# The first block's seven products in another order

## The chip, the cores and the metric

One core of one Trainium2 chip. The metric is the device time of one execution in microseconds (us), from a launch to its end; the median of the runs shown is compared.

## The reference, cut to what matters

The kernel computes one trunk layer for 1024 frames of width 2048: an RMSNorm of x, one input projection, attention over windows of 128 frames, a short gated convolution, one output projection added to x, and a final RMSNorm.

```python
hn = rmsnorm(x, norm_w[l])
proj = einsum('bsd,de->bse', hn, w_in[l])          # 2048 -> 5376 columns
q, k, v, g_attn, h, c_gate, b_gate, g_conv = split(proj, SPLIT_POINTS)
attn = swa_sink_attention(q, k, v, sinks[l], rel_bias)
conv = short_gated_conv(h, c_gate, b_gate, conv_w[l], conv_b[l])
mixed = concatenate([attn * silu(g_attn), conv * silu(g_conv)])
x = x + einsum('bse,ed->bsd', mixed, w_out[l])
return rmsnorm(x, final_norm_w)
```

Everything is float32. What the change touches is the first of eight blocks, which makes `g_attn` (1024 columns) from `hn`.

## The kernel before

**Blocks and products.** All projections are done in eight blocks of 1024 output columns (the second one, QKV, has 1280). A block is a 2 x 2 times 2 x 2 product of halves, done by seven products in place of eight (a Strassen-like scheme in Winograd's form): products 1 and 2 take halves of the weights and of x as they are; 3, 5, 6, 7 and 4 take sums and differences of halves. For the weights these are `s1`, `s2`, `s4`, `s3`, for x `t1`, `t2`, `t3`, `t4`, each in four parts (argument q, 0 to 3). All are made by VectorE in place in the buffers `raw` (weights) and `z` (x). `s2(q)` needs `s1(q)`, `s4(q)` needs `s2(q)`, `s3(q)` needs `s4(q)`; likewise `t2` needs `t1`, `t3` needs `t2`, `t4` needs `t3`. Product 5 takes `s1` and `t1`; product 3 `s4` and the x half that `t2` later overwrites; 6 takes `s2` and `t2`; 7 `s3` and `t3`; 4 the weights as they are and `t4`.

**Steps.** A product is four steps, so a block has 28 and the run 224; step n of this text is the n of the code, and S(n) the time at which TensorE begins it. In the first block product 2 is steps 0 to 3, product 1 steps 4 to 7, and (before) 3 is 8 to 11, 6 is 12 to 15, 7 is 16 to 19, 5 is 20 to 23, 4 is 24 to 27. A step takes two slices of 128 rows, over four output tiles of 128 x 512 (five in QKV), with three matmuls each, since every operand is split into a high and a low float32r part: 24 matmuls (30 in QKV). The three matmuls are high by high, high by low, low by high.

**The splitting.** For each step ScalarE copies the two x slices (`x_hi`, indices 2n and 2n+1, L1007) and the weights (`w_hi`, L976), and VectorE subtracts to get the low parts (`x_lo`, L1349, and `w_lo`, L1336). These go into rings: three steps of weights (`w_ring`), five slices of x (`x_main`). In step n the two engines make `x(2n+3)`, `w(n+2)` and `x(2n+4)`; the ring lets `x(2n+3)` begin only when step n-1 is done, and TensorE needs `x_lo(2n+1)` and `w_lo(n)` to begin step n.

**Order by hand.** Each engine runs one list of instructions in program order; a loop over the steps and four quarters of each says what goes where. Tables at the top place the first block's other work: `S1_AT`, `S24_AT` (`s2` and `s4` together), `B21_AT`, `PARK_AT`, `PLACE1_AT`, `TURN1_AT`, `T1_AT`; `late` shifts `t2`, `t3`, `t4`; `s3` runs from step 12. An engine that waits in this list holds up everything behind it.

**x in the first block.** The first block also makes x itself: TensorE transposes raw x into banks (`turn_x0`, `turn_x1`), and VectorE (`place_0`, `t1_from_turn`) and ScalarE (`place_1`, L1046) move it to `z`. The first step after product 1 waits in `wait_bank` for all eight `place_1` and all eight `t1`. Every x slice of the first block from step 4 on is stored to `x_park` in DRAM by GpSimd's queue (L499), the first steps' slices by `park_hi`, `park_lo`, `store_park` (eight jobs, `PARK_AT`), and the following five blocks load x from there, one DMA of 1024 KB a step (`load_x`, L557). `load_x` of steps 28 and 29 goes to `x_far`.

**Banks.** Products 6 and 7 go on in the banks of product 1, so tile t of product 7 waits until VectorE has read product 6's tile t. Product 3 has banks of its own in the first block. After 2, 3 and 7 ScalarE copies the banks to `e` (`copy_out`, L1100); after 1, 6, 5, 4 VectorE adds or subtracts them (`sums`); product 5's tiles take two instructions each (L1500, L1502).

**The SP queue.** SyncE issues all loads in one list: the next block's weights into `raw` (16 DMAs of 512 KB a block, each when its part of `raw` is free, that is after a `w_lo`), `load_more` (four DMAs of 512 KB, `x_raw`: the extra 256 columns of QKV, needed at step 26 by `more_hi` and then `more_lo`, L1529), `store_gate` (1024 KB each), `load_x`. `load_more` goes into the space of x's low half, so it waits for the last `x_lo` of product 7. `tanh_gate` and `silu_gate` finish the gates, four pairs.

Of the kernel before, what the change touches and what calls it, by code (L numbers as in the profile page):

```python
# [9 lines left out]
ALU = mybir.AluOpType  # L10
# [44 lines left out]
BLOCKS = 8  # L55
ORDER = [(2, 1, 3, 6, 7, 5, 4)] + [(2, 1, 6, 7, 5, 3, 4)] * 5 + [(1, 2, 3, 6, 7, 5, 4), (2, 1, 6, 7, 5, 3, 4)]
AT = [{p: i for i, p in enumerate(o)} for o in ORDER]
# [13 lines left out]

COPIED = [(o[0], 3, 7) if b in ON_CHIP else (o[0], 6, 7) for b, o in enumerate(ORDER)]
ADDED = [(o[1], 6, 5, 4) if b in ON_CHIP else (o[1], 5, 3, 4) for b, o in enumerate(ORDER)]

# [18 lines left out]
def copy_count(b, p, t):  # L93
    return sum(3 * w for w in WIDE[:b]) + COPIED[b].index(p) * WIDE[b] + t + 1

# [13 lines left out]
def _banks():  # L109
    held, free, loose = {}, [0, 1, 2, 3, 4, 5], []  # L110
    for b in range(BLOCKS):
        if b == CONV0:
            free = [k for k in free + loose if k != 5]
            loose = []
        elif b == OUT0:
            free = free + loose + [5, 6, 7]
            loose = []
        for p in ORDER[b]:
            if (b, p) == (GATES, 3):
                free = free + [6, 7]  # L120
            if (b, p) == (QKV, 2):
                free = [k for k in free + loose if k < 6]
                loose = []
            goes_on = {6: 1, 7: 6}.get(p)
            if p == 3 and b not in ON_CHIP:
                goes_on = 5
            mine = []
            for t in range(WIDE[b]):
                if goes_on:
                    k = BANK[b, goes_on, t]  # L130
                else:
                    if t > 0 and loose:
                        free.append(loose.pop(0))
                    if not free:
                        free.append(loose.pop(0))
                    k = free.pop(0)
                BANK[b, p, t] = k
                BANK_BEFORE[b, p, t] = held.get(k)
                held[k] = (b, p, t)
                mine.append(k)  # L140
            free += loose
            loose = []
            if not (p in (1, 6) or (p == 5 and b not in ON_CHIP)):
                loose = mine
# [72 lines left out]
W_TABLED = 10  # L217
S1_AT = {(5, 0): 0, (7, 0): 1, (7, 2): 2, (8, 0): 3}
S24_AT = {(6, 1): 0, (7, 1): 1, (7, 3): 2, (8, 2): 3}
X_HI_AT = {(1, 0): (4, 5), (2, 0): (6, 7), (3, 2): (8, 9), (4, 0): (10,),  # L220
# [28 lines left out]
def build(nc, x, x_t, col_params, w_in, sinks, w_out, rel_bias, final_norm_w, one_hot, out):  # L249
    ctx = ExitStack()  # L250
    with ctx:
# [39 lines left out]
        squares = [z[:, 1, 2:4, :], raw[:, 1, 12:14, :], e[:, 0, 0:2, :], e[:, 0, 2:4, :]]  # L291
        park_stage = [e[:, i, 2 * j:2 * j + 2, :] for i in (1, 3) for j in range(2)]
        taps = cols[:, 0:(TAPS + 1) * GROUPS].rearrange("p (t g) -> p t g", t=TAPS + 1)
# [212 lines left out]
        def _(sp):  # L506
            def load_raw(b, c, j):

                k = slice(2 * j, 2 * j + 2)
                if b > 0:  # L510
                    p = {(0, 0): 7, (0, 1): 3, (1, 0): 5, (1, 1): 4}[c, j // QP]
                    sp.wait_ge(w_lo_ready, at(b - 1, p, j % QP) + 1)
                if b == GATES:
                    src = w_in_v[:, k, GATE_COL + c * N:GATE_COL + (c + 1) * N]
                elif b == QKV:
                    src = w_in_v[:, k, c * N:(c + 1) * N]
                elif b < OUT0:
                    m = b - CONV0
                    for r in range(2):
                        op = sp.dma_start(raw[:, c, k, r * 2 * P:(r + 1) * 2 * P],  # L520
                                          w_conv_v[:, k, 2 * c + r, m * 2 * P:(m + 1) * 2 * P])
                        if r == 0:
                            op.then_inc(raw_loaded[8 * c + j], 16)
                    op.then_inc(raw_loaded[8 * c + j], 16)
                    return
                else:
                    src = w_out_v[:, k, ((b - OUT0) * 2 + c) * N:((b - OUT0) * 2 + c + 1) * N]
                sp.dma_start(raw[:, c, k, :], src).then_inc(raw_loaded[8 * c + j], 16)
# [201 lines left out]
            for n in range(-3, STEPS):  # L730
# [6 lines left out]
                for quarter in range(4):  # L737
# [11 lines left out]
                    if b == GATES:  # L749
                        if (i, q, quarter) == (4, 3, 1):  # L750
                            store_gate(0, 0, 0)
                        if i == 4 and q >= 2 and quarter in (0, 2):
                            load_more(q - 2, quarter // 2)
# [69 lines left out]
                if n + 2 < STEPS:  # L823
                    b, p, q = place(n + 2)
                    if b + 1 < BLOCKS:
                        if p == 3:
                            load_raw(b + 1, 0, QP + q)
                        elif p == 7:
                            load_raw(b + 1, 0, q)
                        elif p == 5:  # L830
                            load_raw(b + 1, 1, q)
                        elif p == 4:
                            load_raw(b + 1, 1, QP + q)
# [125 lines left out]
        def _(act):  # L959
# [89 lines left out]
            def park_hi(j):  # L1049

                act.wait_ge(b21_ready, j // 2 + 1)
                if j < STAGED:
                    act.wait_ge(x1_turned, KT)
                    act.activation(park_stage[j][:, 0, :].bitcast(F32R), z[:, 0, HK + j, :], ACT.Copy
                                   ).then_inc(park_hi_ready, 1)
                    return
                act.wait_ge(x_lo_ready, x_index(at(GATES, 5, j // 2), j % 2) + 1)
                act.activation(z[:, 1, j, :].bitcast(F32R), z[:, 0, HK + j, :], ACT.Copy).then_inc(park_hi_ready, 1)

            def copy_out(b, p, t):  # L1060

                to = (0, 2, 3)[COPIED[b].index(p)]
                if t == 0:
                    if to == 0:
# [5 lines left out]
                        elif b <= OUT0:  # L1070
                            act.wait_ge(conv_step, conv_count(b - 1, 17))
                        else:
                            act.wait_ge(y_stored[0], 16)
                    elif to == 2:
                        if b == GATES:
# [9 lines left out]
                    else:  # L1085
                        if b == GATES:
                            act.wait_ge(park_stored, 16 * STAGED)
                        elif b == QKV:
# [13 lines left out]
            def tanh_gate(i, half):  # L1102

                to = (1, 0, 0, 0)[i]
                p = (ORDER[GATES][1], 5, 5, 4)[i]
                act.wait_ge(sum_ready, sum_count(GATES, p, 3))
                if i > 0:
                    act.wait_ge(gate_stored[0], 16)
                else:
                    act.wait_ge(park_stored, 16 * 2)  # L1110
                if i > 1:
# [113 lines left out]
            for n in range(STEPS):  # L1225
                b, p, q = place(n)
                i = AT[b][p]
                for quarter in range(4):
# [51 lines left out]
                    if b == GATES:  # L1280
                        if (i, q) == (4, 1) and quarter in (1, 3):
                            tanh_gate(0, quarter // 2)
# [47 lines left out]
        def _(dve):  # L1330
# [142 lines left out]
            def sums(b, p, t):  # L1473
# [21 lines left out]
                elif p == 6:  # L1495
                    dve.wait_ge(copy_ready, copy_count(b, 3, t))
                    dve.tensor_tensor(e2, e2, ps, ALU.add).then_inc(sum_ready, 1)
                elif p == 5 and b in ON_CHIP:
                    dve.wait_ge(copy_ready, copy_count(b, 7, t))
# [11 lines left out]
                else:  # L1511
                    dve.wait_ge(sum_ready, sum_count(b, 5, t))
                    if b == OUT1:
# [3 lines left out]
            def silu_gate(i, half):  # L1517

                at_tanh = (1, 0, 0, 0)[i]
                pair = slice(2 * half, 2 * half + 2)  # L1520
# [185 lines left out]
            for n in range(STEPS):  # L1706
                b, p, q = place(n)
                i = AT[b][p]
                for quarter in range(4):
# [46 lines left out]
                    if b == GATES:  # L1756
# [10 lines left out]
                        if (n, quarter) in PARK_AT:  # L1767
                            park_lo(PARK_AT[n, quarter])
                        if quarter == 1 and 12 <= n < 12 + QP:
                            s3(GATES, n - 12)  # L1770
                    if quarter == 2:
# [11 lines left out]
                    if b in ON_CHIP and quarter == 2:  # L1783
                        l = n % LEN
                        if b == OUT0 and 5 <= l < 5 + QP:
                            t1(b, l - 5)
                        late = 1 if b == GATES else 0
                        if 7 + late <= l < 7 + late + QP:
                            t2(b, l - 7 - late)
                        late = 2 if b == GATES else 0  # L1790
                        if 10 + late <= l < 10 + late + QP:
# [9 lines left out]
                    if b == GATES:  # L1801
                        if (i, q) == (4, 2) and quarter in (1, 3):
                            silu_gate(0, quarter // 2)
# [73 lines left out]
        def _(pe):  # L1877
# [48 lines left out]
            def wait_bank(b, p, t):  # L1926

                was = BANK_BEFORE[b, p, t]
                if b == GATES and p == 3:

# [18 lines left out]
            def product(b, p, kt, t, n, parts=(0, 1, 2)):  # L1949
                bank = banks[:, BANK[b, p, t], :]  # L1950
                w, a = w_ring[:, n % NW, kt % 2, :, :], x_halves(n)[kt % 2]
                goes_on = p in (6, 7) or (p == 3 and b not in ON_CHIP)
                first = kt == 0 and not goes_on
# [140 lines left out]
```

## Time and profile before

| | us |
|---|---|
| median of 3 runs | 1350.67 (1349.51 to 1350.72) |
| the profiled execution | 1351.28 |
| its span (first to last instruction) | 1349.5 |
| TensorE matmul busy | 1329.4 (99% of the span) |
| VectorE, ScalarE, GpSimd busy | 918.9, 539.3, 91.0 |
| mean DMA traffic | 289 GB/s |

The profiled execution is 0.6 us over the median. What TensorE doesn't do in the span is 20 us, most of it in the first 70 us, where x is being made. Times in timelines are us from the span's start.

### The profile page before, as it was taken

How to read it: one execution, taken by the hardware profiler on the slowest of the kernel's cores; microseconds unless marked ns; L12 is line 12 of the kernel's file. 1: busy time of each engine (PE TensorE's matmuls, PEld its weight loads, DVE VectorE, ACT ScalarE, POOL GpSimd, SP SyncE). 2: the span in 40 equal slices, each digit the busy share in tenths (PEclk: the TensorE clock that was granted, in tenths of full speed). 3: DMA queues.
4: the chain of work that ended last, by engine and by line, in shares of the span. 5: the costliest groups of instructions: out<-in, count | busy, mean ns of one | idle time of the engine just before them, and what ended most of it. 6: DMA issues, size and time to landing. Idle time of an engine off the chain costs nothing.

```text
span 1349.5 us, 16546 instructions
## 1 busy us (share of the span) xinstructions
PE 1329.4 (99%) x6022; PEld 1098.9 (81%) x6022; DVE 918.9 (68%) x1142; ACT 539.3 (40%) x939; POOL 91.0 (7%) x153
## 2 busy tenths in 40 slices
PE   9999999999999999999999999999999999999997
PEld 7778888888878888888888888878888888888886
DVE  5898876324477458984589855998439896665376
ACT  7754532322232433434334343343423444321454
POOL 1222311000000000000000000000000221100001
PEclk9999999999999999999999999999999999999999
DMA  9778995998878999879998799987998888899768
GB/s 364 282 274 290 405 377 173 304 308 309 314 252 247 285 292 292 246 220 312 296 291 250 225 290 288 288 256 236 300 330 300 319 274 274 288 313 356 279 253 308
DMA packets 205056, 390.02 MB, mean 289 GB/s; under 512 B 78992, under 2 KB 128176, under 8 KB 183344
## 3 DMA queue, kind: packets, MB, share of 16 engines
q1 hardware_dynamic: 185376, 321.83, 72.9%
q0 software_dynamic: 18304, 62.92, 12.7%
q10 hardware_dynamic: 1296, 4.22, 0.8%
q8 instruction: 48, 0.79, 0.2%
q14 instruction: 32, 0.26, 0.1%
HBM read 294.18 MB, written 98.93 MB: 291 GB/s over the span
## 4 chain that ended last, share of the span: by engine, by line
PE 88%; DVE 5%; issue 3%; DMA 2%; ACT 1%; SPq 1%; POOL 0%; DVEq 0%; ACTq 0%; POOLq 0%
PE banks L1962 84%; PE banks L1985 1%; PE banks L1997 1%; DMA qkv_park<-e 1%; DMA raw<-in_w_in_dram 1%; DVE w_ring L1336 1%; PE banks L2006 1%; PE banks L2007 1%; DVE raw L1426 1%; DMA x_far<-x_park 0%; DVE e L1515 0%; DVE z L1398 0%; DVE x_main L1349 0%; DVE raw L1432 0%; ACT z L1207 0%
## 5 line engine op out<-in xcount | busy, mean ns | idle before, releaser
L1962 PE MATMUL banks<-x_main,w_ring 128*128 128x512 f32 x2352 | 551.7, 392 | 4.2 <-DVE x_main L1349 2.5
L1962 PEld LDWEIGHTS banks<-x_main,w_ring 128*128 128x128 f32 x2352 | 438.9, 188 | 95.6 <-issue 5.5
L976 ACT ACTIVATE w_ring<-raw 128x1024 fp32r<-128x1024 f32 x223 | 235.5, 1056 | 555.1 <-PE banks L1962 542.9
L1336 DVE TENSOR_TENSOR w_ring<-raw,w_ring 128x1024 fp32r<-128x1024 f32 x223 | 273.0, 1224 | 217.9 <-ACT w_ring L976 217.7
L1962 PE MATMUL banks<-x_far,w_ring 128*128 128x512 f32 x1680 | 393.4, 391 | 2.0 <-DMA x_far<-x_park 1.9
L1962 PEld LDWEIGHTS banks<-x_far,w_ring 128*128 128x128 f32 x1680 | 313.0, 188 | 66.7 <-issue 2.1
L1962 PE MATMUL banks<-w_ring,x_main 128*128 128x512 f32 x1008 | 230.6, 389 | 0.8 <-DVE x_main L1349 0.8
L1962 PEld LDWEIGHTS banks<-w_ring,x_main 128*128 128x128 f32 x1008 | 189.1, 188 | 40.6 <-issue 1.2
L499 POOL DMA_DIRECT2D x_park<-x_main x104 | 56.1, 540 | 1016.8 <-DVE x_main L1349 1016.8
L1007 ACT ACTIVATE x_main<-z 128x512 fp32r<-128x512 f32 x104 | 64.9, 624 | 129.2 <-issue 102.3
L1349 DVE TENSOR_TENSOR x_main<-z,x_main 128x512 fp32r<-128x512 f32 x104 | 71.5, 687 | 41.0 <-ACT x_main L1007 41.0
L1962 PE MATMUL banks<-w_ring,x_far 128*128 128x512 f32 x336 | 77.9, 389 | 0.5 <-issue 0.5
L1962 PEld LDWEIGHTS banks<-w_ring,x_far 128*128 128x128 f32 x336 | 63.0, 188 | 13.9 <-issue 0.8
L1100 ACT ACTIVATE e<-banks 128x512 f32<-128x512 f32 x92 | 54.7, 597 | 46.0 <-PE banks L1962 45.2
L1153 ACT ACTIVATE probs<-logits,small 128x129 f32<-128x129 f32 x128 | 50.0, 393 | 47.1 <-DVE small L1581 47.0
L1569 DVE SCALAR_TENSOR_TENSOR logits<-banks,bias 128x512 f32<-128x512 f32 (+1 forms) x32 | 21.5, 672 | 45.4 <-PE banks L1985 45.3
L1432 DVE TENSOR_TENSOR raw<-raw 128x1024 f32<-128x1024 f32 x32 | 41.2, 1288 | 1.1
L1438 DVE TENSOR_TENSOR raw<-raw 128x1024 f32<-128x1024 f32 x32 | 39.2, 1224 | 2.9
L1444 DVE TENSOR_TENSOR raw<-raw 128x1024 f32<-128x1024 f32 x32 | 39.1, 1221 | 0.4
L1426 DVE TENSOR_TENSOR raw<-raw 128x1024 f32<-128x1024 f32 x32 | 38.9, 1217 | 0.0
L1505 DVE TENSOR_TENSOR e<-e,banks 128x512 f32<-128x512 f32 x24 | 16.4, 685 | 27.6 <-PE banks L1962 14.3
L1494 DVE TENSOR_TENSOR e<-e,banks 128x512 f32<-128x512 f32 x32 | 21.4, 683 | 17.6 <-PE banks L1962 17.5
(153 smaller groups left out, 858.2 us busy)
## 6 DMA issues: line engine op xcount, KB each, us to landing
x_far<-x_park SPq DMA_DIRECT2D x84, 1024.0 KB, 7.5
x_main<-x_park SPq DMA_DIRECT2D x84, 1024.0 KB, 7.3
x_park<-x_main POOLq DMA_DIRECT2D x104, 512.0 KB, 5.6
raw<-in_w_in_dram SPq DMA_DIRECT2D x130, 256.0 KB, 5.9
raw<-in_w_out_dram SPq DMA_DIRECT2D x32, 512.0 KB, 6.1
raw<-in_w_in_dram SPq DMA_DIRECT2D x31, 512.0 KB, 11.8
q_cur<-qkv_park SPq DMA_DIRECT2D x64, 128.0 KB, 5.8
z<-mix_park SPq DMA_DIRECT2D x16, 512.0 KB, 7.8
```

Source lines behind the costliest of these rows:

```text
L499: engine.dma_start(x_park[0 if n < LEN else 1, n % LEN, :, i, :], x_main[:, k, :, :].rearrange("p a c -> p (a c)").bitcast(F32)).then_inc( ...
L976: act.activation(w_ring[:, n % NW, :, 0, :], raw[:, c, k:k + 2, :], ACT.Copy).then_inc(w_hi_ready, 1)
L1007: act.activation(x_halves(n)[i][:, 0, :], z[:, h, kt16, :], ACT.Copy, scale=scale).then_inc(x_hi_ready, 1)
L1100: act.activation(e_tile(b, to, t), banks[:, BANK[b, p, t], :], ACT.Copy).then_inc(copy_ready, 1)
L1153: op = act.activation(probs[:, j, :], logits[u % 2][:, j, :], ACT.Exp, bias=row_min[:, j:j + 1], scale=-1.0, accum_out=row_sum[:, j:j + 1])
L1336: dve.tensor_tensor(w_ring[:, n % NW, :, 1, :], raw[:, c, k:k + 2, :], w_ring[:, n % NW, :, 0, :], ALU.subtract).then_inc(w_lo_ready, 1)
L1349: dve.tensor_tensor(half[:, 1, :], z[:, h, kt16, :], half[:, 0, :], ALU.subtract).then_inc(x_lo_ready, 1)
L1426: dve.tensor_tensor(raw[:, 1, k, :], raw[:, 1, k, :], raw[:, 1, high, :], ALU.add).then_inc(s1_ready, 1)
L1432: dve.tensor_tensor(raw[:, 0, k, :], raw[:, 1, k, :], raw[:, 0, k, :], ALU.subtract).then_inc(s2_ready, 1)
L1438: dve.tensor_tensor(raw[:, 0, high, :], raw[:, 0, high, :], raw[:, 0, k, :], ALU.subtract).then_inc(s4_ready, 1)
L1444: dve.tensor_tensor(raw[:, 0, k, :], raw[:, 1, high, :], raw[:, 0, k, :], ALU.subtract).then_inc(s3_ready, 1)
L1962: op = pe.matmul(bank, left, right, start=(first and i == 0), stop=(kt == HK - 1 and i == 2), skip_group_check=goes_on)
```

## The change

Product 5 moves from steps 20 to 23 to steps 8 to 11; 3, 6 and 7 each move four steps later (3 is 12 to 15, 6 is 16 to 19, 7 is 20 to 23). Product 5 now gets the banks that 3 had, and 3 goes on in them. ScalarE copies after 2, 5, 3, 7; VectorE adds after 1, 6, 7, 4, and after 7 it takes one instruction a tile, between two parts of `e`. `s2`/`s4`, `s3`, `t2`, `t3`, `t4` and the gates move later. The loads of `raw` for QKV are tied to other products, and the second half's first four no longer wait for steps 20 to 23. `load_more` now waits for the last `x_lo` of steps 20 to 23, and stands four steps later in the list.

```diff
-ORDER = [(2, 1, 3, 6, 7, 5, 4)] + [(2, 1, 6, 7, 5, 3, 4)] * 5 + [...]
+ORDER = [(2, 1, 5, 3, 6, 7, 4)] + [(2, 1, 6, 7, 5, 3, 4)] * 5 + [...]
-COPIED = [(o[0], 3, 7) if b in ON_CHIP else (o[0], 6, 7) for b, o in enumerate(ORDER)]
-ADDED = [(o[1], 6, 5, 4) if b in ON_CHIP else (o[1], 5, 3, 4) for b, o in enumerate(ORDER)]
+COPIED = [(2, 5, 3, 7) if b == GATES else (o[0], 3, 7) if b == OUT0 else (o[0], 6, 7) ...]
+ADDED = [(1, 6, 7, 4) if b == GATES else (o[1], 6, 5, 4) if b == OUT0 else (o[1], 5, 3, 4) ...]
...
-            if (b, p) == (GATES, 3):
+            if (b, p) == (GATES, 5):
                 free = free + [6, 7]
...
-            if p == 3 and b not in ON_CHIP:
+            if p == 3 and b != OUT0:
                 goes_on = 5
...
-S1_AT = {(5, 0): 0, (7, 0): 1, (7, 2): 2, (8, 0): 3}
-S24_AT = {(6, 1): 0, (7, 1): 1, (7, 3): 2, (8, 2): 3}
+S1_AT = {(5, 0): 0, (7, 0): 1, (7, 2): 2, (9, 0): 3}
+S24_AT = {(9, 2): 0, (10, 2): 1, (11, 2): 2, (12, 2): 3}
...
-        park_stage = [e[:, i, 2 * j:2 * j + 2, :] for i in (1, 3) for j in range(2)]
+        park_stage = [e[:, 3, 2 * j:2 * j + 2, :] for _ in range(2) for j in range(2)]
...
                     sp.wait_ge(w_lo_ready, at(b - 1, p, j % QP) + 1)
+                    if b == QKV and (c, j // QP) == (1, 0):
+                        sp.wait_ge(s2_ready, j + 1)
...
-                        if (i, q, quarter) == (4, 3, 1):
+                        if (i, q, quarter) == (5, 1, 1):
                             store_gate(0, 0, 0)
-                        if i == 4 and q >= 2 and quarter in (0, 2):
+                        if i == 5 and q >= 2 and quarter in (0, 2):
                             load_more(q - 2, quarter // 2)
...
-                        elif p == 5:
+                        elif p == (6 if b == GATES else 5):
                             load_raw(b + 1, 1, q)
...
-                to = (1, 0, 0, 0)[i]
-                p = (ORDER[GATES][1], 5, 5, 4)[i]
+                to = (3, 0, 0, 0)[i]
+                p = (1, 7, 6, 4)[i]
...
-                        if (i, q) == (4, 1) and quarter in (1, 3):
+                        if (i, q) == (4, 3) and quarter in (1, 3):
                             tanh_gate(0, quarter // 2)
...
+                elif p == 7:
+                    dve.wait_ge(copy_ready, copy_count(b, 7, t))
+                    dve.tensor_tensor(e1, e1, e3, ALU.add).then_inc(sum_ready, 1)
...
-                        if quarter == 1 and 12 <= n < 12 + QP:
-                            s3(GATES, n - 12)
+                        if quarter == 1 and 16 <= n < 16 + QP:
+                            s3(GATES, n - 16)
...
-                        late = 1 if b == GATES else 0
+                        late = 4 if b == GATES else 0
                         if 7 + late <= l < 7 + late + QP:
                             t2(b, l - 7 - late)
-                        late = 2 if b == GATES else 0
+                        late = 6 if b == GATES else 0
                         if 10 + late <= l < 10 + late + QP:
                             t3(b, l - 10 - late)
...
-                        if (i, q) == (4, 2) and quarter in (1, 3):
+                        if (i, q) == (5, 0) and quarter in (1, 3):
                             silu_gate(0, quarter // 2)
...
-                if b == GATES and p == 3:
+                if b == GATES and p == 5:
                     pe.wait_ge(x1_placed, HK)
                     pe.wait_ge(t1_ready, HK)
```

`t4` keeps its place (steps 18 to 21), as do `b21` (steps 10, 13, 18, 19; L1406) and the parking jobs; the first four parking jobs now share one quarter of `e`.

## Rows read from the trace of the kernel before

**Rows 1.** The page's first part: busy us, share, instructions of each engine.

```profile
PE 1329.4 (99%) x6022; PEld 1098.9 (81%) x6022; DVE 918.9 (68%) x1142; ACT 539.3 (40%) x939; POOL 91.0 (7%) x153
```

**Rows 2.** Waits of TensorE, 0 to 175 us: total, times, longest.

```profile
PE banks L1962 <- DVE x_main L1349: 2.5, 1, 2.5
```

**Rows 3.** ScalarE's timeline at 66 us: start, length, line, idle before.

```profile
66.13 1.06 ACT L976 ACTIVATE w_ring<-raw 128x1024 fp32r<-128x1024 f32 x1 [2.86 <-DVE raw L1438]
...
68.76 1.26 ACT L1046 ACTIVATE z<-banks,cols 128x512 f32<-128x512 f32 x2
```

**Rows 4.** TensorE's timeline at the same place.

```profile
70.23 19.99 PE L1962 MATMUL banks<-x_main,w_ring 128*128 128x512 f32 x80 [2.51 <-DVE x_main L1349]
```

**Rows 5.** Windows: busy us (instructions) of each engine, granted clock, DMA share, GB/s.

```profile
66.80:70.20 3.40, 0.92 (x5) 0.42 (x4) 3.40 (x5) 3.40 (x7) 0.80 (x2) 1.00 0.79 295
70.20:73.60 3.40, 3.37 (x8) 2.73 (x9) 3.30 (x4) 0.67 (x2) 0.26 (x1) 0.52 0.74 229
...
100.00:110.00 10.00, 10.00 (x45) 8.26 (x44) 9.74 (x13) 3.57 (x6) 2.13 (x4) 1.00 0.49 186
...
150.00:160.00 10.00, 10.00 (x46) 8.28 (x45) 8.52 (x13) 4.37 (x8) 4.30 (x8) 1.00 1.04 411
```

**Rows 6.** VectorE's timeline in step 7, s2 and s4 among it.

```profile
63.55 1.22 DVE L1432 TENSOR_TENSOR raw<-raw 128x1024 f32<-128x1024 f32 x1
64.87 1.23 DVE L1438 TENSOR_TENSOR raw<-raw 128x1024 f32<-128x1024 f32 x1
66.02 0.68 DVE L1494 TENSOR_TENSOR e<-e,banks 128x512 f32<-128x512 f32 x1
66.61 0.68 DVE L1349 TENSOR_TENSOR x_main<-z,x_main 128x512 fp32r<-128x512 f32 x1
67.22 1.22 DVE L1426 TENSOR_TENSOR raw<-raw 128x1024 f32<-128x1024 f32 x1
68.35 0.68 DVE L1494 TENSOR_TENSOR e<-e,banks 128x512 f32<-128x512 f32 x1
```

**Rows 7.** VectorE's timeline in steps 18 and 26: t4, b21, silu; more_lo.

```profile
131.15 1.22 DVE L1471 TENSOR_TENSOR z<-z 128x1024 f32<-128x1024 f32 x1
132.28 1.41 DVE L1406 SCALAR_TENSOR_TENSOR z<-z,cols,scratch 128x512 f32<-128x512 f32 x2
133.61 1.22 DVE L1522 SCALAR_TENSOR_TENSOR e<-e 128x1024 f32<-128x1024 f32 x1
...
178.97 1.21 DVE L1529 TENSOR_TENSOR xw<-x_raw,xw 128x1024 fp32r<-128x1024 f32 x1
```

**Rows 8.** ScalarE's x_hi at the start of steps 13 and 14.

```profile
99.37 0.63 ACT L1007 ACTIVATE x_main<-z 128x512 fp32r<-128x512 f32 x1 [2.91 <-issue]
...
104.81 0.63 ACT L1007 ACTIVATE x_main<-z 128x512 fp32r<-128x512 f32 x1 [3.34 <-issue]
```

**Rows 9.** Issues of the SP queue: start, length, line.

```profile
128.03 1.90 SPq L534 DMA_DIRECT2D x_raw<-in_w_in_dram  x2
...
139.18 7.42 SPq L528 DMA_DIRECT2D raw<-in_w_in_dram  x1
```

**Rows 10.** DMA queues, packets, MB, share: 152.6 to 185 us, then 145 to 175.

```profile
q0 software_dynamic: 1983, 6.95, 53.0%
q1 hardware_dynamic: 2416, 6.35, 50.4%
...
q1 hardware_dynamic: 2739, 4.77, 41.5%
```

**Rows 11.** load_x of step 28, then of 29: its issue, and us to landing.

```profile
L557 SPq DMA_DIRECT2D x_far<-x_park x1: 339/339/339, 166.8 to 166.8; - x1
...
DMA to landing us min/median/max: 10.0/10.0/10.0
...
L557 SPq DMA_DIRECT2D x_far<-x_park x1: 332/332/332, 172.0 to 172.0; - x1
...
DMA to landing us min/median/max: 15.0/15.0/15.0
```

More of the change, by code:

```diff
@@ L55 @@
 BLOCKS = 8
-ORDER = [(2, 1, 3, 6, 7, 5, 4)] + [(2, 1, 6, 7, 5, 3, 4)] * 5 + [(1, 2, 3, 6, 7, 5, 4), (2, 1, 6, 7, 5, 3, 4)]
+ORDER = [(2, 1, 5, 3, 6, 7, 4)] + [(2, 1, 6, 7, 5, 3, 4)] * 5 + [(1, 2, 3, 6, 7, 5, 4), (2, 1, 6, 7, 5, 3, 4)]
 AT = [{p: i for i, p in enumerate(o)} for o in ORDER]
@@ L68 @@
 TAIL = 3
-COPIED = [(o[0], 3, 7) if b in ON_CHIP else (o[0], 6, 7) for b, o in enumerate(ORDER)]
-ADDED = [(o[1], 6, 5, 4) if b in ON_CHIP else (o[1], 5, 3, 4) for b, o in enumerate(ORDER)]
+COPIED = [(2, 5, 3, 7) if b == GATES else (o[0], 3, 7) if b == OUT0 else (o[0], 6, 7) for b, o in enumerate(ORDER)]
+ADDED = [(1, 6, 7, 4) if b == GATES else (o[1], 6, 5, 4) if b == OUT0 else (o[1], 5, 3, 4) for b, o in enumerate(ORDER)]
 QKV_KEYS = (True, False, True, False)
@@ L93, in copy_count @@
 def copy_count(b, p, t):
-    return sum(3 * w for w in WIDE[:b]) + COPIED[b].index(p) * WIDE[b] + t + 1
+    return sum(len(c) * w for c, w in zip(COPIED[:b], WIDE)) + COPIED[b].index(p) * WIDE[b] + t + 1
 def sum_count(b, p, t):
@@ L142, in _banks @@
             loose = []
-            if not (p in (1, 6) or (p == 5 and b not in ON_CHIP)):
+            if not (p in (1, 6) or (p == 5 and b != OUT0)):
                 loose = mine
@@ L1053, in park_hi @@
                     act.wait_ge(x1_turned, KT)
+                    if j > 1:
+                        act.wait_ge(park_stored, 16 * 2)
                     act.activation(park_stage[j][:, 0, :].bitcast(F32R), z[:, 0, HK + j, :], ACT.Copy
@@ L1057, in park_hi @@
                 act.wait_ge(x_lo_ready, x_index(at(GATES, 5, j // 2), j % 2) + 1)
+                act.wait_ge(t2_ready, j // 2 + 1)
                 act.activation(z[:, 1, j, :].bitcast(F32R), z[:, 0, HK + j, :], ACT.Copy).then_inc(park_hi_ready, 1)
             def copy_out(b, p, t):
-                to = (0, 2, 3)[COPIED[b].index(p)]
+                to = ((0, 1, 2, 3) if b == GATES else (0, 2, 3))[COPIED[b].index(p)]
                 if t == 0:
@@ L1073, in copy_out @@
                             act.wait_ge(y_stored[0], 16)
+                    elif to == 1:
+                        act.wait_ge(x1_turned, KT)
                     elif to == 2:
@@ L1086, in copy_out @@
                         if b == GATES:
-                            act.wait_ge(park_stored, 16 * STAGED)
+                            act.wait_ge(gate_ready, 2)
                         elif b == QKV:
@@ L1109, in tanh_gate @@
                 else:
-                    act.wait_ge(park_stored, 16 * 2)
+                    act.wait_ge(park_stored, 16 * STAGED)
                 if i > 1:
@@ L1497, in sums @@
                     dve.tensor_tensor(e2, e2, ps, ALU.add).then_inc(sum_ready, 1)
-                elif p == 5 and b in ON_CHIP:
+                elif p == 7:
+                    dve.wait_ge(copy_ready, copy_count(b, 7, t))
+                    dve.tensor_tensor(e1, e1, e3, ALU.add).then_inc(sum_ready, 1)
+                elif p == 5 and b == OUT0:
                     dve.wait_ge(copy_ready, copy_count(b, 7, t))
@@ L1511, in sums @@
                 else:
-                    dve.wait_ge(sum_ready, sum_count(b, 5, t))
+                    dve.wait_ge(sum_ready, sum_count(b, 7 if b == GATES else 5, t))
                     if b == OUT1:
@@ L1517, in silu_gate @@
             def silu_gate(i, half):
-                at_tanh = (1, 0, 0, 0)[i]
+                at_tanh = (3, 0, 0, 0)[i]
                 pair = slice(2 * half, 2 * half + 2)
@@ L1951, in product @@
                 w, a = w_ring[:, n % NW, kt % 2, :, :], x_halves(n)[kt % 2]
-                goes_on = p in (6, 7) or (p == 3 and b not in ON_CHIP)
+                goes_on = p in (6, 7) or (p == 3 and b != OUT0)
                 first = kt == 0 and not goes_on
```

## The prediction, made before the changed kernel was run

> **What bounds the kernel now.** I read the busy shares first: TensorE's matmuls fill 99% of the span [rows 1], and the change neither adds nor removes a matmul. So only TensorE's idle time and its clock can move the total. Next come the waits of TensorE in the first block: the one that the new order can touch is 2.51 us at step 8, from 67.72 to 70.23 [rows 2, 4]. Then the windows around it: while TensorE was idle the granted clock was 1.00, and from the moment it resumed it was 0.52 over 3.4 us, that is 1.2 in place of 2.4 GHz [rows 5]. So the stall costs twice. Eight matmuls were begun in that window where 16 is the normal number, and step 9 can be dated from ScalarE's rows: its x_hi begins 0.24 us after each step does, so step 13 began at 99.13, steps are 5.44 us long [rows 8], and counting back five steps to step 8 at 70.23 leaves 1.7 us that the low clock took. The stall is worth 2.51 + 1.70 = 4.21 us.
>
> Who is late at step 8? The wait names x_lo, but x_lo(17) began at 66.61 and was done by 67.3 [rows 6]. The step also waits for all eight place_1, and the last two ended at 70.02 on ScalarE [rows 3]. They were late because w_hi(9) stands ahead of them and had waited 2.86 us for s4 [rows 3], and s4 was late because VectorE had s1, s2, s4, t1, sums and splitting back to back [rows 6]. VectorE is the engine to watch: 9.74 of 10 us busy even at 100 to 110 [rows 5].
>
> **The step-8 wait goes.** w_hi(9) now needs only s1(1). VectorE sheds s2(0) and s4(0) before step 8, and s2(1), s4(1). A pair is 1.32 + 1.15 = 2.47 us (63.55 to 64.87 to 66.02) [rows 6]. By the rows' spacings s1(1) is done near 61, w_hi(9) runs at about 63, and the last place_1 ends near 67.3, against 67.72 when step 7 is over. x_lo(17) is done by about 65.2. So step 8 begins at 67.7, and with no stall I expect no drop of the clock there: -4.21 us. What is late next is the place_1 chain, with 0.4 us to spare.
>
> **What VectorE gives back, steps 9 to 14.** The four pairs don't vanish; all four now stand in steps 9 to 12. I add up VectorE's list by its spacings: x_lo 0.60, sums 0.60, parking 0.60, w_lo, s1, s3, t2, t3, t4 and a silu half 1.14, a pair 2.47, b21 1.36 [rows 6, 7]. The first x_lo of step n can't begin before S(n) + 0.9 (x_hi 0.24 after the start, 0.63 long) [rows 8]. The same sum with the old order puts t4(0) at 131.05 where the row has 131.15 [rows 7], so I trust it to a few tenths. New order, with S(9) = 73.15:
> - Step 9: x_lo(21) at 74.0, s1(3) to 75.8; w_hi(11) waits for that, so w_lo(11) begins at 77.0; x_lo, then pair 0, to 81.2.
> - Step 10: x_lo(23), w_lo(12) (its w_hi waits for s4(0), 0.6 lost), x_lo, pair 1, b21: to 88.0.
> - Step 11: 2.34 for splitting, two parkings 1.2, pair 2, t2: 7.15, to 95.1.
> - Step 12: x_lo(27) is done at 95.8 where S(13) should be 94.9: TensorE waits 1.0. The rest, with pair 3 and t2(1), lasts to 101.1, so S(14) is 0.5 late again.
> Sum +1.5 us. After this t2 alone remains, and VectorE catches up by step 16.
>
> **Steps 18 to 20.** In the new order s3 and t3 (steps 16 to 19) fall on t4, b21 and the sums of product 6. Step 18 is 2.34 + 1.14 x 3 + 1.36 = 7.1 us. Step 19 is 2.34 + s3, t3, t4 3.42 + b21 1.36 + three sums 1.8 = 8.9 us against 5.44. Product 7 goes on in product 6's banks, so tiles 1, 2, 3 of step 20 wait for sums that end near 136.7, 139.6 and 141.6 where step 20 begins at 134.5 with 1.36 us a tile: waits of 1.0, 1.5 and 0.6, together 3.1 us. x_lo(43) at 142.2 is then just in time for step 21 at 143.0. Before, the same sums ended with at most some tenths against them. Taken off elsewhere: product 5's second sum (4 x 0.60) goes, four ScalarE copies come; ScalarE is 40% busy [rows 1], so they cost nothing unless VectorE's waits on w_hi grow. I cost the other moved parts (silu, tanh, the shared parking buffer) at nothing: between steps 21 and 26 the list has room. Bounds for all VectorE waits: 1.5 if ScalarE and the semaphores are kinder, 6.5 if they lose a few tenths more per product.
>
> Account to step 26: -4.21 + 1.5 + 3.1 = +0.4 us. Step 26 begins at 170.2 against 169.8 before.
>
> **The late transfers.** load_more (4 x 0.52 = 2.1 MB) was issued from 128.03 [rows 9]. Now it waits for x_lo(47) of step 23, which by the list ends at 152.6. From 150 on the DMA engines are full: share 1.04, 411 GB/s, where at 100 to 110 they are half idle, 0.49 [rows 5]. The early issue of raw's loads (near 103) fills that idle stretch, which doesn't help the end. Behind load_more in the same queue stand raw's last loads and load_x(28). What must move from 152.6 until load_x(28) has landed: the POOL queue's stores, 6.95 MB from 152.6 to 185 before [rows 10], of which I take 6.7; on the SP queue about 0.8 left of gate 0 and one raw load (issued 147 to 149), 2.1 of load_more, three raw loads 1.6, load_x 1.05: 5.5 MB. (6.7 + 5.5) / 0.413 MB per us = 29.6 us, and 1.6 us from last byte to landing: 184.0. Before, it was issued at 166.8 and landed 10.0 later, at 176.8, with step 28 at 180.7 [rows 11]: 3.9 us to spare. Now step 28 is due at 181.1 and waits 2.9 us. Bounds: below, the old 10.0 us from an issue at about 168.3, 178.3, no wait at all; above, the SP queue's own old rate, 4.77 MB in 30 us [rows 10]: 5.5 / 0.159 = 34.6 us, 187.2, a wait of 6.1. A wait of 2.9 us is longer than the 2.51 that was followed by the low clock, so I add 1.7 for a second drop. load_x(29) is 2.6 MB later in the queue (gate 1, raw, itself), 6.3 us, 190.3, against step 29 at 184.0 + 6.8 + 1.7 = 192.5: covered. more_lo, before at 178.97 with half a us to spare for step 28 [rows 7], also sits behind load_more and one raw load (s1 of QKV stands ahead of it on VectorE); I put it near 180, inside the same wait.
>
> SP was held 7.42 us at one issue behind the small-row x_raw loads [rows 9], which shows that the queue fills; it delays issues, not the order of the bytes. On order the Trainium skill (DMA: Bandwidth & Descriptors, section "Queues, rings and completion order") says that each DMA engine takes turns between queue rows, packet by packet. That speaks against this change: load_more's short rows take many turns, each beside a longer one of the POOL queue. The sum by bytes would then be too kind to load_x(28), which would land nearer the upper bound than 184.0. No row here separates the two.
>
> **Sum.** At step 28: -4.21 + 4.6 + 2.9 = +3.3, and 1.7 of clock, +5.0 us. Nothing after step 29 is touched. The profiled execution took 1351.28 us (span 1349.5 and 1.8 around it): 1356.3, and as it lies 0.6 over the median, 1355.7.
>
> **Rivals.**
> - *VectorE gives back, the transfers don't.* load_x(28) lands by 181, because the idle DMA time at 100 to 110 let the backlog be smaller. For it: 3.9 us of room. Against: 2.1 MB more are asked of full engines in the last 30 us. Time: 1350.67 + 0.4 = 1351.1.
> - *The gain stays.* The s2/s4 pairs and step 19's pile are absorbed, since the rings hold nearly four us of slack in a steady step (x_hi(29) at 99.4 for a step at 104.6, [rows 8]), and the loads come in time. It decides if VectorE is less than about 1 us late in each place. Time: 1350.67 - 4.2 = 1346.5; with half of the waits 1348.7. Against: the sum above uses up this slack already, and step 19's 8.9 us are 3.5 over.
> - *The queue is worse.* load_x(28) at 187.2 (SP queue's old rate, or turns as above), 6.1 us of wait, one drop of the clock: 0.4 + 6.1 + 1.7 = +8.2, 1358.9.
> - *The change doesn't do what it says*: step 8 still waits since place_1 is late by 1 us. Then the gain is smaller and everything later the same; it ends where the forecast does, since load_x(28) sets the end.
>
> **How the numbers follow.** Forecast 0.50 (1355.7, its own range 1353.4 to 1357.7); transfers in time 0.22; gain stays 0.13; worse queue 0.15. This kernel's measurement can't tell less than 0.2%, 2.7 us. Slower: 0.48 of the forecast and the 0.15 less a bit, 0.61; same: the 0.22 and the edges, 0.26; faster 0.13. Range 1349.5 to 1359.5: it takes in the bounds but for the gain staying whole.
>
> **What would show it.** Right: no wait at step 8 and clock 1.00 at 67 to 75; TensorE waits of about 1 us on x_lo near 95, three waits on product 6's sums near 136 to 142; x_raw issued near 152; the longest wait at step 28, near 181, on x_far, with 0.5 clock behind it. Wrong: no wait at 136 to 142 (VectorE's list mis-sized), or x_far landing before 181 (the DMA sum), or a wait near 67.

## The result, and the profile after

The changed kernel takes 1359.44 us (median of 5 runs, 1358.95 to 1362.86) against 1350.67 of the kernel before in the same rounds (1349.51 to 1350.87). The ratio is 1.0067, 95% interval 1.0055 to 1.0080: slower by 8.8 us. The profiled execution took 1359.31 us, its span is 1357.5 where it was 1349.5: 8.0 us more.

The busy shares after (engine, busy us, share of the span, instructions), beside [rows 1]. As many matmuls as before; only how long TensorE stood still or ran slowly can have changed:

```profile
PE 1331.4 (98%) x6022; PEld 1099.3 (81%) x6022; DVE 915.1 (67%) x1138; ACT 541.0 (40%) x943; POOL 90.7 (7%) x153
```

The x_main wait of 2.5 us [rows 2] is gone, and six others are new: two on x_main, three on VectorE's sums, and the longest at step 28. Here they are in TensorE's timeline after (start, length, line, operation, count, and in brackets the idle time ahead and what ended it). It answers to [rows 4]: where a run of matmuls ended at 67.72 and the next began at 70.23, one run now goes from 64.96 to 95.16, through step 8.

```profile
64.96 30.20 PE L1972 MATMUL banks<-x_main,w_ring 128*128 128x512 f32 x132
96.04 5.71 PE L1972 MATMUL banks<-x_main,w_ring 128*128 128x512 f32 x24 [0.88 <-DVE x_main L1356]
101.98 34.29 PE L1972 MATMUL banks<-x_main,w_ring 128*128 128x512 f32 x150 [0.23 <-DVE x_main L1356]
137.01 1.66 PE L1972 MATMUL banks<-x_main,w_ring 128*128 128x512 f32 x6 [0.75 <-DVE e L1504]
139.88 1.66 PE L1972 MATMUL banks<-x_main,w_ring 128*128 128x512 f32 x6 [1.21 <-DVE e L1504]
141.81 39.74 PE L1972 MATMUL banks<-x_main,w_ring 128*128 128x512 f32 x174 [0.27 <-DVE e L1504]
187.27 7.49 PE L1972 MATMUL banks<-x_far,w_ring 128*128 128x512 f32 x24 [5.72 <-issue]
...
195.96 5.60 PE L1972 MATMUL banks<-x_far,w_ring 128*128 128x512 f32 x24
```

The idle time in brackets runs from the modelled end of the last matmul, which overlaps the next by 0.27 us. From start to start (24 matmuls at 5.44 us), the waits are 1.16 and 0.50 us at steps 13 and 14, 1.03, 1.51 and 0.57 us inside step 20, and 6.01 us at step 28, due at 181.26.

Windows after, around step 8 and from step 28's wait on (window and length; busy us and count of PE, PEld, DVE, ACT, POOL; granted clock; DMA share; GB/s). They answer to [rows 5]:

```profile
66.80:70.20 3.40, 3.40 (x17) 2.81 (x16) 3.40 (x6) 2.59 (x4) 0.53 (x1) 1.00 0.93 328
70.20:73.60 3.40, 3.40 (x17) 2.81 (x16) 1.80 (x3) 0.11 (x1) 1.07 (x2) 1.00 0.75 299
...
181.60:184.40 2.80, 0.00 (x0) 0.00 (x0) 1.48 (x2) 1.06 (x1) 2.16 (x1) 0.98 1.06 400
184.40:187.20 2.80, 0.00 (x0) 0.00 (x0) 2.80 (x4) 0.32 (x1) 0.18 (x1) 0.50 0.99 399
187.20:191.00 3.80, 3.73 (x9) 2.98 (x10) 3.80 (x4) 1.69 (x2) 0.00 (x0) 0.50 1.09 428
```

Full clock at 66.8 to 73.6, where it was 0.52 from 70.2 on. The low level (0.50, 1.2 GHz) now comes at step 28: it began near 184.4, while TensorE stood still, and lasted until about 191.1, that is 3.8 us into the matmuls (the granted clock from 191 to 192 was 0.93). At half speed 3.8 us cost 1.9. Step 28's 24 matmuls and the six behind them start 8.69 us apart from step 29's (187.27 to 195.96) in place of 6.80 [180.80 to 187.60 before]: 1.89 us.

ScalarE's two lines that set step 8, after, beside [rows 3]: w_hi(9) runs at 63.40, and the last two place_1 end at 67.29 in place of 70.02.

```profile
63.40 1.06 ACT L978 ACTIVATE w_ring<-raw 128x1024 fp32r<-128x1024 f32 x1
66.01 1.28 ACT L1048 ACTIVATE z<-banks,cols 128x512 f32<-128x512 f32 x2
```

VectorE at steps 19 and 20 after. The sums that free tiles 1, 2 and 3 (L1504) end at 136.96, 139.83 and 141.75, and what stands between them is s3, t3, t4 and b21:

```profile
135.15 1.21 DVE L1451 TENSOR_TENSOR raw<-raw 128x1024 f32<-128x1024 f32 x1
136.28 0.68 DVE L1504 TENSOR_TENSOR e<-e,banks 128x512 f32<-128x512 f32 x1
136.88 1.21 DVE L1469 TENSOR_TENSOR z<-z 128x1024 f32<-128x1024 f32 x1
138.02 1.21 DVE L1478 TENSOR_TENSOR z<-z 128x1024 f32<-128x1024 f32 x1
139.15 0.68 DVE L1504 TENSOR_TENSOR e<-e,banks 128x512 f32<-128x512 f32 x1
139.75 1.40 DVE L1413 SCALAR_TENSOR_TENSOR z<-z,cols,scratch 128x512 f32<-128x512 f32 x2
141.07 0.68 DVE L1504 TENSOR_TENSOR e<-e,banks 128x512 f32<-128x512 f32 x1
```

The releaser at step 28 is given as "issue", that is, no event the profile can name. SP's timeline shows who it was (time in which SP issues, not in which data move). It answers to [rows 9] and [rows 11]: the small-row x_raw loads begin at 152.80 in place of 128.03, SP is held 11.00 us at one issue behind the first two of them and 7.42 us at the other two, and load_x(28) is issued at 179.28 in place of 166.8. It landed 7.9 us later, at 187.2, and step 28 began at 187.27.

```profile
152.80 2.24 SPq L536 DMA_DIRECT2D x_raw<-in_w_in_dram  x2
155.09 11.00 SPq L530 DMA_DIRECT2D raw<-in_w_in_dram  x1
166.12 7.42 SPq L536 DMA_DIRECT2D x_raw<-in_w_in_dram  x2
173.59 5.58 SPq L530 DMA_DIRECT2D raw<-in_w_in_dram  x2
179.28 0.40 SPq L559 DMA_DIRECT2D x_far<-x_park  x1
```

more_lo, which also sits behind load_more, ran from 178.62 to 179.84 and was not what step 28 waited for.

Now the queues (packets, MB, share of the 16 engines' time), first from 152.8 to 187.2, after; it answers to [rows 10]:

```profile
DMA packets 7774, 13.30 MB, mean 387 GB/s; under 512 B 448, under 2 KB 4544, under 8 KB 7645
q0 software_dynamic: 2153, 7.57, 54.9%
q1 hardware_dynamic: 5620, 5.71, 48.9%
```

And from 155 to 170 us, the time of the small rows; after first, then before:

```profile
q0 software_dynamic: 1511, 5.28, 86.8%
q1 hardware_dynamic: 1398, 0.72, 17.1%
```

```profile
q0 software_dynamic: 1189, 4.15, 67.9%
q1 hardware_dynamic: 1059, 2.04, 35.2%
```

q0 is POOL's queue with the stores, 3.5 KB a packet; q1 is SP's. In this stretch the two queues move about equally many packets. After, SP's packets are 0.5 KB, so it moves 0.72 MB of the 6.0, where it moved 2.04, and everything that SP wants for step 28 stands behind those rows. The Trainium skill (DMA: Bandwidth & Descriptors, section "Queues, rings and completion order") says that each engine takes turns between queue rows, packet by packet. By that rule the short rows lose, and this stretch agrees, with the packets as the profile counts them (one row each): from 158 to 166 us the two queues moved 798 and 796. From 155 to 158 it was 351 and 54, since load_more's rows were hardly moving yet.

The turns hold only while both queues have something to send. From 130 to 146 us, where the kernel before moved its small rows and POOL had issued six stores of 512 KB, SP's queue moved 4368 packets to POOL's 751. The same stretch after shows what left it (before first, then after):

```profile
DMA packets 5121, 6.14 MB, mean 384 GB/s; under 512 B 167, under 2 KB 3679, under 8 KB 5119
q1 hardware_dynamic: 4368, 3.38, 64.0%
q0 software_dynamic: 751, 2.74, 42.6%
```

```profile
DMA packets 1032, 2.98 MB, mean 186 GB/s; under 512 B 95, under 2 KB 95, under 8 KB 1030
q0 software_dynamic: 575, 2.09, 33.8%
q1 hardware_dynamic: 455, 0.87, 20.2%
```

After, the engines stand half empty there, at 186 in place of 384 GB/s. In this stretch 3.2 MB less are moved. A part had been moved before it (10.85 in place of 8.24 MB from 100 to 130 us, raw's early loads), so from 60 to 146 us it is 1.9 MB less (22.73 for 24.63), and these have to move in the full stretch behind.

The stores come later too. POOL's queue from 152.8 to 180.7 us, before and then after:

```profile
q0 software_dynamic: 1956, 6.87, 60.7%
```

```profile
q0 software_dynamic: 2153, 7.57, 67.7%
```

After 180.7 it moves nothing in the changed kernel, so 7.57 MB is all it had. From 146 to 152.8 us it had moved 0.82 MB in place of 1.77: POOL issued its first four stores of 256 KB from 150.65 in place of 147.23 us, having waited in its list for x_lo, which VectorE made late.

From step 8 to step 29, summed start to start: step 7's end 0.24 later, step 8's wait and low clock gone (−2.79 − 1.77 = −4.56), the VectorE waits 1.16 + 0.50 + 1.03 + 1.51 + 0.57 = +4.77, step 28 +6.01, its clock +1.89. Together +8.35; step 29 begins 195.96 − 187.60 = 8.36 us later. That is the whole loss within 0.4 us of the spans' difference.

### The profile page after: what moved, and what is told of

Read it like the earlier page. It is cut to its first block, busy times and chain, and to the rows that moved or that the text cites. A ratio compares the mean times of both kernels' runs of the same rounds, so it can differ in the third digit from the quotient of the medians.

```text
span 1357.5 us, 16551 instructions
## 1 busy us (share of the span) xinstructions
PE 1331.4 (98%) x6022; PEld 1099.3 (81%) x6022; DVE 915.1 (67%) x1138; ACT 541.0 (40%) x943; POOL 90.7 (7%) x153
## 4 chain that ended last, share of the span: by engine, by line
PE 83%; DVE 6%; issue 4%; DMA 4%; ACT 1%; SPq 1%; POOL 0%; DVEq 0%; ACTq 0%; POOLq 0%
PE banks L1972 79%; DMA raw<-in_w_in_dram 2%; PE banks L1995 1%; DVE w_ring L1343 1%; PE banks L2007 1%; DMA qkv_park<-e 1%; PE banks L2016 1%; DVE x_main L1356 1%; PE banks L2017 1%; PE banks L1932 1%; DVE e L1525 0%; DVE raw L1433 0%; DVE raw L1439 0%; DMA x_far<-x_park 0%; ACT w_ring L978 0%
```

## The experiments

The theory that I took into them (T, for turns): 6.0 + 1.9 us come from load_x(28) standing behind load_more, whose 512-byte rows take one turn each beside rows of the stores that are seven times as long. The rivals: (B) the bytes are to blame, moved into a stretch where the DMA engines are full, whatever their rows; (V) VectorE's list costs the time, and the transfers would have been late anyway.

**load_more behind load_x(28)**, three quarters of it, in the changed kernel (the edit shortened; the wait for x_lo moves to the DMA that now goes first):

```diff
-if i == 5 and q >= 2 and quarter in (0, 2): load_more(q - 2, quarter // 2)
+if (i, q, quarter) == (5, 2, 0): load_more(0, 1)
+if (i, q, quarter) == (6, 2, 0): load_more(0, 0)
+if (i, q, quarter) == (6, 3, 0): load_more(1, 0); load_more(1, 1)
```

> The changed kernel, with three of the four load_more DMAs (1.6 of 2.1 MB) behind load_x(28) in the SP queue's list; the first, which step 26 needs, keeps its place. Theory T (turns): the 512-byte rows of load_more, ahead of load_x(28) in one queue, hold it back while GpSimd's queue has stores. Then load_x(28) lands near 181, step 28 waits under 1 us, no drop of the clock there, and of the 8.8 us lost 5.7 + 1.9 come back: about 1351.8 us. Rival R (the wait at step 28 comes from the moved loads of raw or from more_lo): the wait stays over 4 us, 1357 to 1360 us.

Measured 1352.01 us, ratio to the kernel before 1.0013 (1.0004 to 1.0022), 7.4 us less than the changed kernel. TensorE's timeline and SP's issue of load_x(28):

```profile
141.31 39.73 PE L1977 MATMUL banks<-x_main,w_ring 128*128 128x512 f32 x174 [0.28 <-DVE e L1509]
181.36 5.72 PE L1977 MATMUL banks<-x_far,w_ring 128*128 128x512 f32 x24 [0.33 <-issue]
```

```profile
165.92 0.34 SPq L559 DMA_DIRECT2D x_far<-x_park  x1
```

Issued 13.4 us earlier, landed at 181.3; the wait of 5.72 has fallen to 0.33 and the clock stayed up. VectorE's waits ahead are as they were. A smaller wait, 0.59 us on load_x(29), is new at step 29. So the wait at step 28 and its clock hang on load_more's place, 7.4 us by the times. V can't account for more of the net loss than the 1.5 us by which this kernel is slower than the kernel before of its rounds (1350.54): VectorE's 4.8 us of waits are there, and the 4.6 won at step 8 pay for them.

**The same bytes in rows of 2048.** To tell turns from bytes:

```diff
-x_raw[:, c, h*HK:(h+1)*HK, :] <- w_in_v[:, h*HK:(h+1)*HK, K_ROW+c*P : K_ROW+(c+1)*P]
+x_raw[...].rearrange("p (a b) m -> p a (b m)", a=2) <- w_in_v[:, 4*c+2*h : 4*c+2*h+2, 0:N]
```

> The changed kernel; load_more moves the same bytes at the same places of the list, but from 2048-byte rows in place of 512-byte rows (other columns of w_in, so QKV's last 256 columns are computed from other weights). Theory T (turns by packet): a quarter of the packets, so load_x(28) lands 3 to 4 us earlier, near 184, the wait at step 28 falls from 5.7 to 2 to 3 us: about 1355.5 to 1356.5 us. Theory B (only bytes count, as in the prediction's sum): nothing moves, 1359.4 us, wait 5.7 us.

Measured 1357.87 us, 1.0059 (1.0045 to 1.0072). TensorE at step 28, and the queues from 155 to 170 us:

```profile
185.97 7.33 PE L1972 MATMUL banks<-x_far,w_ring 128*128 128x512 f32 x24 [4.60 <-DMA x_far<-x_park]
```

```profile
q0 software_dynamic: 1233, 4.27, 70.8%
q1 hardware_dynamic: 952, 1.85, 32.1%
```

The queues' shares are nearly back at those of before (1.85 MB for SP where it was 0.72), as T says, and yet the wait went down only from 5.72 to 4.60 us. Of the wait, 1.1 us are the short rows; the other 4.6 are there with long ones. The time fell by 1.6 us, with runs that overlap those of the changed kernel. T as I had put it falls, and B holds for most of it: more bytes in the full stretch. All queues together, from 152.8 us to the landing at 185.9:

```profile
DMA packets 4837, 13.55 MB, mean 409 GB/s; under 512 B 448, under 2 KB 448, under 8 KB 4708
```

That is nearly the full rate (0.413) of my sum, where the changed kernel had 387 GB/s. SP was also held less: load_x(28) was issued at 169.29, 10 us sooner than in the changed kernel, and landed only 1.3 us sooner. So the hold of SP is not what made it late. The starving is real but largely made up for: once the stores' queue runs low (69 packets from 178 to 182 us in the changed kernel), SP's queue has the engines almost alone.

**The kernel before, with its load_more late**, two of its four DMAs at step 23 and two at step 24; nothing else of the change (the edit shortened):

```diff
-if i == 4 and q >= 2 and quarter in (0, 2): load_more(q - 2, quarter // 2)
+if (i, q, quarter) in ((5, 3, 0), (6, 0, 0)): load_more(int(i == 6), 0); load_more(int(i == 6), 1)
```

> The kernel before, with load_more alone moved later in the SP queue's list: two DMAs at step 23, two at step 24, so that they are issued near 152 and 158 us as in the changed kernel; the order of the products stays. Theory T: load_x(28) lands after 185, step 28 waits 4 to 6 us, and the clock falls behind it: 1356 to 1359 us. Rival R (it takes the new order): under 1352 us and no wait at step 28 over 1 us.

Measured 1356.07 us, 1.0042 (1.0029 to 1.0054). TensorE at step 28, and SP:

```profile
184.43 8.26 PE L1963 MATMUL banks<-x_far,w_ring 128*128 128x512 f32 x24 [3.36 <-DVE w_ring L1337]
```

```profile
159.99 9.79 SPq L534 DMA_DIRECT2D x_raw<-in_w_in_dram  x2
174.91 0.82 SPq L557 DMA_DIRECT2D x_far<-x_park  x1
```

The wait is a little below what was expected (3.4 for 4 to 6 us). load_x(28) was issued at 174.9 and landed 9.4 later, at 184.3; the splitting that the profile names (L1337) is for step 30 and ended then by chance. So load_more's place alone, with the old order of products and VectorE's old list, costs 5.5 us against the kernel before of its rounds.

**The control: the kernel before with load_more behind.**

> The kernel before, with three of its four load_more DMAs behind load_x(28), as in the first of these experiments. In the kernel before load_x(28) had 3.9 us to spare, so all theories expect nothing: 1350.2 to 1350.9 us. It is the control for the versions with that edit: if it gains over 1 us, their gain isn't the new order's.

Measured 1351.01 us, 1.0000 (0.9989 to 1.0010): the same edit as in the first experiment, its first DMA one product earlier. Step 28 begins without a wait. In the kernel before the move gains nothing, so the 7.4 us of the first experiment are a repair of the change's own loss.

**VectorE's lists evened**, load_more left late:

```diff
-S24_AT = {(9, 2): 0, (10, 2): 1, (11, 2): 2, (12, 2): 3}
+S24_AT = {(8, 2): 0, (9, 2): 1, (10, 2): 2, (11, 2): 3}
-if quarter == 1 and 16 <= n < 16 + QP: s3(GATES, n - 16)
+if quarter == 1 and 15 <= n < 15 + QP: s3(GATES, n - 15)
-late = 6 if b == GATES else 0        # t3
+late = 4 if b == GATES else 0
```

> The changed kernel with VectorE's list thinned where it was late: the s2/s4 pairs one step earlier (steps 8 to 11), s3 one step and t3 two steps earlier. By VectorE's list the waits of 0.9, 0.2 and 2.2 us (steps 13, 14, 20) shrink to 0.5 together, and step 26 begins 4 us earlier. Theory T: load_more is issued 4 us earlier too, so load_x(28) lands near 183 and step 28 still waits 5 us with the clock's fall behind it: about 1355 to 1356 us. Rival D (the DMA engines' backlog sets the end of step 27 whatever VectorE does): load_x(28) lands at 187 as before, 1359.4 us.

Measured 1357.63 us, 1.0048 (1.0035 to 1.0060), with runs from 1354.63 to 1358.37; the profile is of the lowest.

```profile
95.54 81.89 PE L1972 MATMUL banks<-x_main,w_ring 128*128 128x512 f32 x360 [0.49 <-DVE x_main L1356]
183.42 7.09 PE L1972 MATMUL banks<-x_far,w_ring 128*128 128x512 f32 x24 [5.99 <-issue]
```

360 matmuls in one run: the three waits of step 20 and that of step 14 are gone. Step 28 was due earlier and waits 5.99 us, as long as before the edit: load_more waits for x_lo in SP's list, so it was issued 4.4 us sooner in this execution (148.40), load_x(28) 4.0 us sooner (175.28), and it landed near 183.3 in place of 187.2. That refutes D for this execution, which is 4.8 us below the changed kernel's median. The five runs lie in two groups, 1354.63 and 1355.20, and 1357.63 to 1358.37. The median gains only 1.8 us and is above the 1355 to 1356 expected; what the slower three did differently no trace shows.

**Both: lists evened, load_more behind.**

> Both of the two edits together on the changed kernel: VectorE's list thinned (s2/s4 and s3 a step earlier, t3 two steps earlier) and three of the four load_more DMAs behind load_x(28). Theory T (the 4.2 us of step 8 are won, VectorE's list and the queue behind load_more each take their part, and they add): VectorE's waits 0.5 us, wait at steps 28 and 29 together under 1.5 us, no drop of the clock: 1347 to 1348.5 us, 2 to 3 us faster than before. Rival D (the DMA engines' backlog fixes the time of step 28 or 29 whatever comes earlier): steps 28 and 29 wait 4 us longer than with load_more behind alone, 1352 us.

Measured 1348.71 us, 0.9985 (0.9976 to 0.9993): 2.2 us faster than before, 3.3 less than with load_more behind alone (the two medians are of different rounds; by the ratios it is 3.8). That is what the lists' 4 us of VectorE's waits are worth with load_more behind. The profiled execution is the slowest of the 11, 1351.55, but its waits are as theory T says: 0.49 us at step 13, and at step 28

```profile
178.61 5.72 PE L1977 MATMUL banks<-x_far,w_ring 128*128 128x512 f32 x24 [0.26 <-issue]
```

**Step 8 alone**: in the kernel before, w_hi(9) issued behind place_1 (W_HI_AT `(7, 2): 9` to `(8, 0): 9`), so that the old order keeps its products and step 8 isn't held.

> The kernel before with one table entry moved: w_hi(9) stands after the last place_1 (step 8 in place of step 7), so nothing of the order changes but step 8 needn't wait for s4. Theory V (behind the wait stood VectorE's full list): the 2.5 us wait at step 8 is replaced by waits of about 1.4 and 1.6 us at steps 9 and 10 on x_lo; with the clock's 1.7 us not lost, 1349 to 1349.5 us; with it lost, 1350.5. Rival (the wait was place_1's alone): all 4.2 us won, 1346.4 us.

Measured 1350.34 us, 0.9992 (0.9983 to 1.0001), not told apart from no change:

```profile
75.01 5.73 PE L1962 MATMUL banks<-x_main,w_ring 128*128 128x512 f32 x24 [1.45 <-DVE x_main L1349]
82.09 98.28 PE L1962 MATMUL banks<-x_main,w_ring 128*128 128x512 f32 x432 [1.35 <-DVE x_main L1349]
```

Step 8's wait is gone and two of 1.45 and 1.35 us stand at the next steps: VectorE was late in any case, the stall moved. The clock stayed at 1.00 all through, which saves 1.77 us. But from start to start the two waits are 1.72 and 1.64 us, 0.57 more than the 2.79 at step 8, so 1.2 us are left. By step 29 the trace shows 0.7 of them, and the medians differ by 0.6, with an interval from 2.3 us faster to 0.1 slower.

**The best version**: both edits, and t2 one step later (late = 5).

> As the run with both edits, with t2 one more step later (steps 12 to 15), which by VectorE's list takes away the last wait of 0.5 us at step 13. Theory T: 0.5 us faster than that run, 1346.5 to 1348 us. Rival (the half us is taken back at steps 28 and 29 by the transfers): the same time as that run.

Measured 1346.95 us, 0.9968 (0.9957 to 0.9979), faster than both kernels. All of TensorE's timeline from 64.8 to step 28:

```profile
64.78 111.79 PE L1977 MATMUL banks<-x_main,w_ring 128*128 128x512 f32 x492
178.16 5.72 PE L1977 MATMUL banks<-x_far,w_ring 128*128 128x512 f32 x24 [1.58 <-issue]
```

492 matmuls without a wait, step 28 1.6 us late and no low clock. Step 29 begins at 185.08, 2.5 us ahead of before and 10.9 ahead of the changed kernel. The gain over the version before it, 1.8 us, is more than the 0.5 that I had put on record.

## Why the prediction was right or wrong

- *What bounds it, and step 8* (forecast −4.21, measured −4.56): right. TensorE's run goes through step 8 at full clock, and place_1 ended at 67.29, forecast 67.3. The difference is the 0.28 us of overlap that the idle column hides, and 0.07 of clock.
- *VectorE gives back, steps 13 and 14* (forecast 1.0 and 0.5, measured 1.16 and 0.50): right.
- *Step 20's tiles* (forecast 1.0, 1.5, 0.6; sums ending 136.7, 139.6, 141.6; measured 1.03, 1.51, 0.57; 136.96, 139.83, 141.75): right. A list of one engine's spacings gave five waits to within 0.2 us.
- *The late transfers*: this is the step that failed. load_more was issued at 152.80 (forecast 152.6), and the place of the wait and its object were right, but load_x(28) landed at 187.2 instead of 184.0, so the wait was 6.01 us and not 2.9. Two terms of the sum (6.7 + 5.5 MB) / 0.413 + 1.6 us were mis-sized. The first is the stores: I took 6.7 of the 6.95 MB of before, and there were 7.57, since stores that waited for VectorE's late x_lo came later (read from POOL's timeline). The 0.87 MB are 2.1 us at 0.413. The second is the rate: 387 GB/s in place of 413. The long-rows experiment parts the two. With 7.53 MB of stores and 409 GB/s, load_x(28) landed at 185.9, so the stores' term accounts for those 1.9 us; the short rows account for the 1.3 us from there to 187.2. SP's own 5.5 MB were not too few: up to 1.6 us before the landing that queue had moved 5.10 MB, and 5.40 with long rows. The 1.6 us from last byte to landing stand in no row and no run, and the sum as written gives 183.7, not 184.0.
- *more_lo and load_x(29)*: covered, as forecast. load_x(29) landed at 193.5, 2.5 us ahead of step 29.
- *The second low clock* (forecast 1.7, measured 1.89): right that it came, near in size partly by luck. Other waits at step 28 cost 1.49 to 2.66 us, by when the low stretch began.
- *The sum*: +5.0 forecast, 8.8 measured by the medians, 8.4 by the traces up to step 29. The wait at step 28 is 3.1 us over, its clock 0.2, VectorE's waits 0.2, step 7 ended 0.2 later, and step 8 gave 0.35 more. The rival "the queue is worse" had 187.2, a wait of 6.1 and 1358.9 us, and I gave it 0.15. Its number came true, its mechanism in part, and the exact 187.2 is luck. It took SP's old rate of 0.159 MB per us, which was 5.71 MB in 34.4 us or 0.166, and left out the 1.6 us that the forecast added. The turns that I named beside it are 1.1 us of the wait. Before, too, the two queues moved nearly equal packets in most stretches (160 and 160 from 162 to 164 us), which would have told me of the turns but not of the stores.
- *The rivals on the other side*: "the transfers come in time" is refuted by the changed kernel and holds only where load_more stands behind (1352.01 us, forecast 1351.1). "The gain stays" came true only in the best version, which has evened lists and load_more behind: 1346.95, forecast 1346.5.

What stays open: why the runs with evened lists alone fall into two groups, and the half us by which the step-8 edit gains less in the trace than its waits and clock say. That VectorE's lateness is what made the stores late is read from POOL's waits for x_lo; no run changes it alone.

## What to carry to other kernels

When a load moves to a later place in a queue, what counts is what stands behind it there. Count anew what every queue will move in the new stretch, in the new kernel: here the full rate over all bytes came out right to 1% with long rows, and what was wrong was to take the other queue's old bytes, though the change had made its stores later. Short rows beside long ones came on top, as 1.3 us. A late engine may cost twice, in its own waits and in the transfers that wait for it; the second was read here from one trace and not tested alone. Here the largest gain came from the transfer that was waited for last (7.4 us), then from the lists (3.3), then from t2's place (1.8). Leave short-row loads in stretches where the other queue has little to send, or put them behind the load that a step waits for.

## What the runs showed of the hardware

- While both queues had work they moved nearly as many packets as each other: 798 and 796 (after, 158 to 166 us), with mean sizes seven to one, and 1344 and 1347 (long rows, 158 to 176). Where POOL's queue had less they did not (751 and 4368, before, 130 to 146). So short rows are cheap for their queue in the one stretch and costly in the other.
- Short rows lowered the total rate: 387 GB/s from 152.8 us to the landing after, 409 with the same bytes in long rows.
- The issuing engine is held: SP stood 11.00 us at one issue, and 7.42 and 9.79 us at two issues together, near load_more's 512-byte rows. That need not delay the data: with long rows load_x(28) was issued 10 us sooner and landed 1.3 us sooner.
- The low clock did not follow the length of a wait simply. Waits of 2.51, 3.36, 4.60, 5.72 and 5.99 us were each followed or accompanied by it, and waits of 1.58, of 1.45 and 1.35, and three of 0.75, 1.21 and 0.27 within 5 us were not. Its price from start to start was 1.77, 2.66, 1.73, 1.89 and 1.49 us. With the waits of 3.36, 5.72 and 5.99 us it began while TensorE stood still, so that a part of the low stretch cost nothing.
